# Values and gates of two blocks as 512 wide matmuls over paired weights, and a spread of roots by one product a head

## The chip, the cores and the metric

The kernel runs on one core of a Trainium2 chip. The metric is the device time of one launch in microseconds, lower is better. TensorE multiplies, VectorE and ScalarE empty its PSUM banks and prepare operands, GpSimd takes inverse roots and some sums, and SyncE issues most loads.

## The reference

Two transformer blocks over 512 tokens of width 1024, in float32, one after the other. What the change touches of them:

```python
# first block: gated linear attention (GLA), 4 heads of 256 values, 256 context tokens
q, k, v, r, glr = split(h @ w_in)
o = head_rms_norm(scan forwards + scan backwards)      # per head of 256
y = (o * silu(r)) @ w_out                              # r: the scan gates
# second block: the mixer
u_pool, q, k, v, g = split(rmsnorm(h) @ w_in)
a = pool_mixer(u_pool)
o = retention(rope(q), rope(k), v)                     # 4 heads of 128, chunks of 128
o = o * rsqrt(mean(o * o, axis=-1) + EPS) * gain       # a root per token and head
h = h + concat([a, silu(g) * o]) @ w_out
```

Around these stand the norms, the modulation of the first block and three gated feed-forward layers (width 2816), which take most of the time.

## The kernel before, in words

**Precision by parts.** Each large product is computed from two parts of either operand. ScalarE rounds a raw weight unit w_raw (128 x 8 x 256, slot 0 or 1) to its upper part w_hi (`split_hi`, L1190), VectorE subtracts for the lower part w_lo (`split_lo`, L1606), and activations lie as a_hi and a_lo. `mm3` (L505) issues three matmuls: upper by upper, upper by lower, lower by upper. A matmul here is a weight load of 128 x 128 and the columns that move past it.

**Most units** (`unit`, L526) have the weights stationary and 512 tokens moving, so that the output has features on partitions. **Three kinds have tokens stationary** and 256 features moving, for an output with tokens on partitions: the GLA values (`v_unit`, L696, not changed), the GLA scan gates r (`r_half`, L750) and the mixer's values (L1039 to L1049). A tile is 128 tokens by 256 features: 8 steps k of 3 matmuls of 256 columns, 24 in all. Two tiles share a PSUM bank (512 float32 columns), one in each half.

**Scan gates.** Each of the four heads of GLA is one round of a loop (L806 to L829). TensorE turns the keys, computes tiles 0 and 1 of the gates into bank 2 (`r_half(h, 0)`), the scores, the key products of blocks 0 and 1, tiles 2 and 3 into bank 3 (`r_half(h, 1)`), the key product of block 2, turns the gated output of the head before and computes the output of this one. ScalarE takes the silu of a whole bank into sr (`silu_half`, L1358), both at the end of its round and ahead of `split_hi`; that frees the bank. VectorE multiplies sr into the normed output (`gate_o`, L1900), merges the scores (`merged_scores`, L1878) and carries the states (`states`, L1888), on which TensorE waits ahead of block 2.

**Mixer's values.** TensorE runs ten units of w_in in order: two for the pool input, two for k, two for q, two for v, two for g. After each, VectorE scales or rotates the output in PSUM (`rotate`, L2245: four instructions for each of two banks). VectorE's queue around the values is an order written out by hand (L2270 to L2322): rotate(4), split_lo(1), rotate(5), split_lo(0), the decayed operands of two retention heads (`ret_inputs`, L2281), split_lo(1). rotate(5) belongs to unit 5, the last of q. The values' two units n = 0, 1 fill banks 2n and 2n + 1, two tiles each. Unit 0 waits for rotate(4), unit 1 for rotate(5). ScalarE copies each tile into vr, scaled by the token's root (L1540 to L1547), and splits the next weights behind each unit. TensorE then waits for all eight copies (L1124), computes the scores and turned keys of head 0 and the first of the gate chunks.

**Retention roots.** GpSimd raises the 16 mean squares of a partition (4 heads, 4 token tiles) to the power -1/2 (L482). TensorE spreads them over the partitions by 16 matmuls of 128 columns, with the root as a broadcast stationary operand and the identity moving (L1158 to L1163). They are plain float32, for which the profile shows two passes each. VectorE multiplies them into gr (L2360), ScalarE and VectorE split the result, and TensorE uses it from `mix_part(0, range(4, KD))` on. Elsewhere in the kernel a spread is one matmul of 512 columns: all ones stationary, and moving a row of four diagonals, which VectorE makes (`diagonal`, L1637; `broadcast`, L554).

Of the kernel before, what the change touches and what calls it, by code (L numbers as in the profile page):

```python
# [7 lines left out]
ALU = mybir.AluOpType  # L8
# [113 lines left out]
def build(nc, a):  # L122
    with ExitStack() as ctx:  # L123
# [27 lines left out]
        w_hi = [place(f"w_hi{s}", [P, KD, UC], F32R) for s in range(2)]  # L151
        w_lo = [place(f"w_lo{s}", [P, KD, UC], F32R) for s in range(2)]
# [73 lines left out]
        st = tmp[2]  # L226
        ret_q, ret_k, ret_p = ([tmp[j], dec_k[i]] for i, j in enumerate((0, 1, 3)))
# [31 lines left out]
        masks_set, reset_set = sem("masks_set"), sem("reset_set")  # L259
# [41 lines left out]
        cst_done = sem("context_state_copied")  # L301
        o_hi_done, o_lo_done = sem("o_hi_done"), sem("o_lo_done")
# [189 lines left out]
        def _(pe):  # L492
# [257 lines left out]
            def r_half(h, half):  # L750

                s, b = h % 2, 2 + half
                if half == 0:
                    pe.wait_ge(lo_done[s], cnt.next(lo_done[s]))
                take(b)
                for j in range(2):
                    t = 2 * half + j
                    for k in range(KD):
                        m = mm3(bank[b][:, j * DV:(j + 1) * DV],
                                (a_hi[:, k, t * P:(t + 1) * P], a_lo[:, k, t * P:(t + 1) * P]),  # L760
                                (w_hi[s][:, k], w_lo[s][:, k]), k == 0, k == KD - 1)
                m.then_inc(ready[b], 1)
# [276 lines left out]
            for n in range(2):  # L1039
                pe.wait_ge(lo_done[n], cnt.next(lo_done[n]))  # L1040
                pe.wait_ge(roped, cnt.upto(roped, CPU * (n + 3)))
                for b in (2 * n, 2 * n + 1):
                    for j in range(2):
                        t = 2 * (b % 2) + j
                        for k in range(KD):
                            m = mm3(bank[b][:, j * UC:(j + 1) * UC],
                                    (a_hi[:, k, t * P:(t + 1) * P], a_lo[:, k, t * P:(t + 1) * P]),
                                    (w_hi[n][:, k], w_lo[n][:, k]), k == 0, k == KD - 1)
                    m.then_inc(ready[b], 1)  # L1049
# [108 lines left out]
            pe.wait_ge(root_done, 12)  # L1158
            for h in range(HR):
# [1372 lines left out]
```

## Time and profile before

| | us |
|---|---|
| median of 3 runs | 1614.9 |
| lowest and highest | 1614.07, 1618.32 |
| the profiled execution: its time | 1615.48 |
| its span | 1613.7 |
| TensorE busy in it | 1598.7 (99%) |
| VectorE, ScalarE, GpSimd busy | 843.4, 497.7, 119.8 |
| mean granted clock of TensorE | 0.996 |

The difference between the execution's time and its span lies outside what the engines' records cover. A matmul's row gives a start and a modelled duration, which overlaps the next: the distance of two starts is what one costs. In a timeline a row is start, duration, engine, line, operation, output and inputs, and in brackets the idle time ahead of it with what ended it. A granted clock of 1.00 is 2.4 GHz, 0.50 is 1.2 GHz.

### The profile page before, as it was taken

Reading aid. Unit: us, or ns where it says so; the run is one execution under the profiler, and the core shown is the slowest. Engines: PE = TensorE matmul, PEld = TensorE weight load, DVE = VectorE, ACT = ScalarE, POOL = GpSimd, SP = SyncE. Lnnn points to the kernel's source line nnn. Section 1 sums busy time; section 2 is a strip of 40 time slices with the busy share of each in tenths; the row PEclk is TensorE's granted clock in tenths of the full one; section 3 lists DMA queues with packets and bytes.
Section 4 is the critical chain, followed back from the end, with each engine's and each line's share of the span. In section 5 each row is a group of like instructions: output and inputs, shape, how many; then the busy total and the mean of one; then the engine's idle time right before and its main releaser. Section 6 shows DMA issues by size and latency. Waiting matters only on the chain.

```text
span 1613.7 us, 19892 instructions
## 1 busy us (share of the span) xinstructions
PE 1598.7 (99%) x8095; PEld 1359.1 (84%) x8095; DVE 843.4 (52%) x1032; ACT 497.7 (31%) x571; POOL 119.8 (7%) x106
## 2 busy tenths in 40 slices
PE   8999999999999999999999999999999999999998
PEld 6899999888888888888888888888988888888887
DVE  5897754674334344584544444346457445444444
ACT  4553264532222233441221222321223212222222
POOL 0100000020000000000000003135006000000000
PEclk9999999999999999999999999999999999999999
DMA  9544511212222222322222223332212222222332
GB/s 384 183 167 157 209 53 53 79 61 96 104 104 80 90 88 89 113 85 109 80 102 104 79 84 104 99 144 105 79 53 78 105 104 83 99 104 67 96 98 79
DMA packets 30361, 171.38 MB, mean 106 GB/s; under 512 B 3168, under 2 KB 5472, under 8 KB 16608
## 3 DMA queue, kind: packets, MB, share of 16 engines
q1 hardware_dynamic: 25952, 153.80, 27.3%
q0 software_dynamic: 4352, 16.78, 3.1%
q8 instruction: 41, 0.67, 0.2%
q14 instruction: 16, 0.13, 0.0%
HBM read 168.47 MB, written 2.10 MB: 106 GB/s over the span
## 4 chain that ended last, share of the span: by engine, by line
PE 96%; DMA 2%; DVE 1%; issue 0%; SPq 0%; ACT 0%; POOL 0%; POOLq 0%; DVEq 0%
PE bank L503 95%; DMA mod_w<-in_mod 2%; DVE mod_sum L1629 0%; PE bank L803 0%; SPq L346 0%; PE bank L747 0%; ACT w_hi L1193 0%; PE bank L1072 0%; PE bank L693 0%; SPq L349 0%; DVE y_ffn L2405 0%; ACT tmp L1396 0%; POOL root L408 0%; POOLq L123 0%; DVE qd L1982 0%
## 5 line engine op out<-in xcount | busy, mean ns | idle before, releaser
L1608 DVE TENSOR_TENSOR w_lo<-w_raw,w_hi 128x2048 fp32r<-128x2048 f32 x142 | 327.8, 2308 | 378.1 <-ACT w_hi L1193 378.0
L503 PE MATMUL bank<-a_hi,w_hi 128*128 128x512 f32 x1245 | 486.8, 391 | 0.0
L503 PE MATMUL bank<-a_hi,w_lo 128*128 128x512 f32 x1245 | 484.5, 389 | 0.0
L503 PE MATMUL bank<-a_lo,w_hi 128*128 128x512 f32 x1245 | 484.5, 389 | 0.0
L1193 ACT ACTIVATE w_hi<-w_raw 128x2048 fp32r<-128x2048 f32 x144 | 275.5, 1913 | 556.3 <-PE bank L503 556.1
L503 PEld LDWEIGHTS bank<-a_hi,w_hi 128*128 128x128 f32 x1245 | 233.8, 188 | 49.9 <-issue 1.9
L503 PEld LDWEIGHTS bank<-a_hi,w_lo 128*128 128x128 f32 x1245 | 233.7, 188 | 48.8
L503 PEld LDWEIGHTS bank<-a_lo,w_hi 128*128 128x128 f32 x1245 | 233.8, 188 | 48.1 <-issue 0.5
L503 PE MATMUL bank<-g_hi,w_hi 128*128 128x512 f32 (+1 forms) x544 | 210.4, 387 | 0.0
L503 PE MATMUL bank<-g_lo,w_hi 128*128 128x512 f32 (+1 forms) x544 | 210.0, 386 | 0.0
L503 PE MATMUL bank<-g_hi,w_lo 128*128 128x512 f32 (+1 forms) x544 | 210.0, 386 | 0.0
L503 PEld LDWEIGHTS bank<-g_hi,w_lo 128*128 128x128 f32 x544 | 102.5, 188 | 20.7
L503 PEld LDWEIGHTS bank<-g_lo,w_hi 128*128 128x128 f32 x544 | 102.6, 189 | 20.5
L503 PEld LDWEIGHTS bank<-g_hi,w_hi 128*128 128x128 f32 x544 | 102.6, 189 | 20.4
L503 PE MATMUL bank<-w_hi,a_hi 128*128 128x256 f32 x320 | 91.9, 287 | 0.0
L408 POOL TENSOR_TENSOR root<-col,power 128x4 f32<-128x4 f32 (+2 forms) x15 | 17.3, 1154 | 996.3 <-DVE col L1635 809.7
L503 PE MATMUL bank<-w_hi,a_lo 128*128 128x256 f32 x320 | 90.5, 283 | 0.0
L503 PE MATMUL bank<-w_lo,a_hi 128*128 128x256 f32 x320 | 90.5, 283 | 0.0
L1459 ACT ACTIVATE tmp<-tmp 128x512 f32<-128x512 f32 x44 | 27.7, 632 | 175.9 <-DVE tmp L2137 175.9
L2143 DVE TENSOR_TENSOR tmp<-bank,roots 128x512 f32<-128x512 f32 x44 | 30.4, 692 | 98.4 <-PE bank L503 98.4
L2137 DVE TENSOR_TENSOR tmp<-bank,roots 128x512 f32<-128x512 f32 x43 | 29.5, 688 | 88.1 <-PE bank L503 85.2
L503 PEld LDWEIGHTS bank<-w_hi,a_hi 128*128 128x128 f32 x320 | 61.2, 191 | 0.2
(299 smaller groups left out, 1604.2 us busy)
## 6 DMA issues: line engine op xcount, KB each, us to landing
w_raw<-in_ffn_in SPq DMA_DIRECT2D x66, 1024.0 KB, 4.8
w_raw<-in_ffn_out SPq DMA_DIRECT2D x24, 768.0 KB, 4.2
mod_raw<-in_mod POOLq DMA_DIRECT2D x16, 1024.0 KB, 5.5
w_raw<-in_ffn_out SPq DMA_DIRECT2D x24, 640.0 KB, 3.9
w_raw<-in_gla_in SPq DMA_DIRECT2D x12, 1024.0 KB, 4.8
w_raw<-in_mix_in SPq DMA_DIRECT2D x10, 1024.0 KB, 4.9
mod_w<-in_mod SPq DMA_DIRECT2D x8, 1024.0 KB, 18.8
w_raw<-in_gla_out SPq DMA_DIRECT2D x4, 1024.0 KB, 4.7
```

What stands on the lines that cost most here:

```text
L408: nc.gpsimd.tensor_tensor(root4[:, c0:c0 + n], col4[:, c0:c0 + n], power[:, 0:n], ALU.pow).then_inc(root_done, 1)
L503: return pe.matmul(out, lhs, rhs, start=first, stop=last, skip_group_check=True)
L1193: nc.scalar.activation(flat(w_hi[s]), flat(w_raw[s]), ACT.Copy).then_inc(hi_done[s], 1)
L1459: nc.scalar.activation(tmp[c][:], tmp[c][:], ACT.Silu).then_inc(silu_done, 1)
L1608: V.tensor_tensor(flat(w_lo[s]), flat(w_raw[s]), flat(w_hi[s]).bitcast(F32), ALU.subtract).then_inc(lo_done[s], 1)
L2137: V.tensor_tensor(tmp[c][:], gate, roots[:], ALU.mult).then_inc(gate_scaled, 1)
L2143: V.tensor_tensor(tmp[2 + c][:], bank[2 + c][:], roots[:], ALU.mult).then_inc(up_scaled, 1)
```

## The change

w_hi and w_lo of a slot become the two halves of one tensor, w_two. A new function computes a tile of tokens with two matmuls a step instead of three: the upper activations stationary and 512 columns moving, which are the upper weights' 256 and then the lower weights' 256, and the lower activations stationary with the upper weights' 256 added into the bank's second half. Upper by upper then lies in the first half of a bank and the rest in the second, so that a tile fills a bank. ScalarE copies the first half to SBUF and VectorE adds the second.

The gates use banks 2 and 3 in turn, and tiles wait for VectorE's adds (r_added); the silu runs in SBUF. The values' units use banks 2n and 2n + 1 in turn, and tiles 2 and 3 wait for VectorE's add of tiles 0 and 1 (free). TensorE's wait for the copies of the values goes, and one for the four banks comes behind the first scores. The roots of retention are spread by one product of 512 columns a head, from diagonals that VectorE makes.

```diff
-        w_hi = [place(f"w_hi{s}", [P, KD, UC], F32R) for s in range(2)]
-        w_lo = [place(f"w_lo{s}", [P, KD, UC], F32R) for s in range(2)]
+        w_two = [place(f"w_two{s}", [P, 2, KD, UC], F32R) for s in range(2)]
+        w_hi, w_lo = ([w_two[s][:, j] for s in range(2)] for j in range(2))
...
+            def tile_of_tokens(b, s, t):
+                for k in range(KD):
+                    hi, lo = (x[:, k, t * P:(t + 1) * P] for x in (a_hi, a_lo))
+                    mm(bank[b][:].rearrange("p (w e) -> p w e", w=2), hi, w_two[s][:, :, k], k == 0, False)
+                    m = mm(bank[b][:, UC:2 * UC], lo, w_hi[s][:, k], False, k == KD - 1)
+                return m
...
             def r_half(h, half):
...
-                take(b)
                 for j in range(2):
                     t = 2 * half + j
-                    for k in range(KD):
-                        m = mm3(bank[b][:, j * DV:(j + 1) * DV],
...
-                m.then_inc(ready[b], 1)
+                    if h or t >= 2:
+                        pe.wait_ge(r_added, PAIRS * h + t - 1)
+                    else:
+                        take(2 + j)
+                        filled[2 + j] = False
+                    tile_of_tokens(2 + j, s, t).then_inc(ready[2 + j], 1)
...
             for n in range(4):
...
+                if n == 0:
+                    pe.wait_ge(r_added, PAIRS * HG)
...
-                for b in (2 * n, 2 * n + 1):
-                    for j in range(2):
-                        t = 2 * (b % 2) + j
-                        for k in range(KD):
-                            m = mm3(bank[b][:, j * UC:(j + 1) * UC],
...
-                    m.then_inc(ready[b], 1)
+                for t in range(RCH):
+                    b = 2 * n + t % 2
+                    if t >= 2:
+                        pe.wait_ge(free[b], cnt.next(free[b]))
+                    tile_of_tokens(b, n, t).then_inc(ready[b], 1)
...
-            pe.wait_ge(v_copied, cnt.next(v_copied, 8))
             ret_scores_of(0)
+            for b in range(4):
+                pe.wait_ge(free[b], cnt.next(free[b]))
             gate_chunk(0)
...
             mix_part(1, range(3))
-            pe.wait_ge(root_done, 12)
-            for h in range(HR):
-                for t in range(RCH):
-                    c = RCH * h + t
-                    m = mm(bank[4 + h][:, t * P:(t + 1) * P], root4[:, c:c + 1].to_broadcast([P, P]), ident[:], True, True)
-                m.then_inc(roots_ready, 1)
+            broadcast(4, T, ret_diag[0])
+            broadcast(5, T, ret_diag[1])
             mix_part(1, (3,))
+            broadcast(6, T, ret_diag[2])
+            broadcast(7, T, ret_diag[3])
             mix_part(0, range(4, KD))
...
# ScalarE
+            def upper_half(h, half):
+                for j in range(2):
+                    act.wait_ge(ready[2 + j], cnt.next(ready[2 + j]))
+                    nc.scalar.activation(sr[h % 2][:, 2 * half + j], bank[2 + j][:, 0:DV], ACT.Copy).then_inc(r_left, 1)
...
             def silu_half(h, half):
-                b = 2 + half
-                act.wait_ge(ready[b], cnt.next(ready[b]))
...
+                act.wait_ge(r_added, PAIRS * h + 2 * half + 2)
+                x = sr[h % 2][:, 2 * half:2 * half + 2]
+                nc.scalar.activation(x, x, ACT.Silu)
...
                     middle_decays(h + 1)
+                upper_half(h, 0)
                 block_states(h, 1)
...
                 silu_half(h, 0)
+                upper_half(h, 1)
+                split_hi(h % 2)
                 silu_half(h, 1)
-                split_hi(h % 2)
...
# VectorE
+            def gate_sums(h, half):
+                for j in range(2):
+                    t = 2 * half + j
+                    dve.wait_ge(r_left, PAIRS * h + t + 1)
+                    x = sr[h % 2][:, t]
+                    V.tensor_tensor(x, x, bank[2 + j][:, DV:2 * DV], ALU.add).then_inc(r_added, 1)
...
                     gate_o(h - 1)
+                gate_sums(h, 0)
                 merged_scores(h)
...
                     o_lower(h - 1)
+                gate_sums(h, 1)
                 split_lo(h % 2)
...
             rotate(5)
+            def values_added(n, tiles):
+                for t in tiles:
+                    x = vr[:, t, n * UC:(n + 1) * UC]
+                    b = 2 * n + t % 2
+                    dve.wait_ge(v_copied, cnt.next(v_copied))
+                    V.scalar_tensor_tensor(x, bank[b][:, UC:2 * UC], root4[:, t:t + 1], x, ALU.mult, ALU.add).then_inc(free[b], 1)
+            values_added(0, range(RCH))
             split_lo(0)
...
             ret_inputs(0)
+            values_added(1, (0, 1))
             ret_inputs(1)
+            values_added(1, (2, 3))
             split_lo(1)
...
+            for h in range(HR - 1):
+                diagonal(ret_diag[h], RCH, RCH * h)
             for h in range(HR):
                 dve.wait_ge(roots_ready, cnt.next(roots_ready))
                 V.tensor_tensor(gr[:, h], gr[:, h], bank[4 + h][:], ALU.mult).then_inc(scaled, 1)
-                if h:
+                if h == 0:
+                    diagonal(ret_diag[HR - 1], RCH, RCH * (HR - 1))
+                else:
                     head_lower(h - 1)
```

ScalarE's copies of the values change with the tiles (256 columns from a bank's first half, the same scale). Two semaphores of the mask set-up are replaced by the general step semaphore, with the same waits.

## Rows read from the trace of the kernel before

**Rows 1.** The page: busy time by engine, and the chain's shares by engine

```profile
PE 1598.7 (99%) x8095; PEld 1359.1 (84%) x8095; DVE 843.4 (52%) x1032; ACT 497.7 (31%) x571; POOL 119.8 (7%) x106
...
PE 96%; DMA 2%; DVE 1%; issue 0%; SPq 0%; ACT 0%; POOL 0%; POOLq 0%; DVEq 0%
```

**Rows 2.** The chain in order of time: start, duration, what

```profile
191.98 0.76 DVE mod_sum L1629
...
231.67 15.89 PE bank L503 x124
...
332.73 359.33 PE bank L503 x1584
...
1151.79 1.13 PE bank L503 x8
...
1153.35 7.02 PE bank L503 x38
```

**Rows 3.** TensorE's timeline, the mixer's values: matmuls 1, 2 and 192

```profile
1127.62 0.28 PE L503 MATMUL bank<-w_hi,a_hi 128*128 128x256 f32 x1
1127.73 0.28 PE L503 MATMUL bank<-w_lo,a_hi 128*128 128x256 f32 x1
...
1150.53 0.28 PE L503 MATMUL bank<-w_hi,a_lo 128*128 128x256 f32 x1
```

**Rows 4.** VectorE's timeline beside the mixer's values

```profile
1129.77 2.29 DVE L1608 TENSOR_TENSOR w_lo<-w_raw,w_hi 128x2048 fp32r<-128x2048 f32 x1 [2.81 <-ACT w_hi L1193]
...
1137.15 0.69 DVE L2260 TENSOR_TENSOR qr<-qr,tmp 128x512 f32<-128x512 f32 x1
1142.01 2.29 DVE L1608 TENSOR_TENSOR w_lo<-w_raw,w_hi 128x2048 fp32r<-128x2048 f32 x1 [4.17 <-ACT w_hi L1193]
1144.21 0.69 DVE L2284 TENSOR_TENSOR tmp<-qr,decay 128x512 f32<-128x512 f32 x1
1144.82 0.69 DVE L2284 TENSOR_TENSOR tmp<-kr,decay 128x512 f32<-128x512 f32 x1
```

**Rows 5.** ScalarE's timeline beside the mixer's values

```profile
1127.82 1.92 ACT L1193 ACTIVATE w_hi<-w_raw 128x2048 fp32r<-128x2048 f32 x1 [8.96 <-PE bank L503]
...
1139.33 0.84 ACT L1545 ACTIVATE vr<-bank,root 128x256 f32<-128x256 f32 x2 [4.92 <-PE bank L503]
1140.06 1.91 ACT L1193 ACTIVATE w_hi<-w_raw 128x2048 fp32r<-128x2048 f32 x1
```

**Rows 6.** The tile sr: VectorE's three-operand form (ns: shortest, median, longest)

```profile
L1908 DVE SCALAR_TENSOR_TENSOR sr<-bank,root,sr x16: 472/476/485, 212.8 to 280.1; 128x256 f32<-128x256 f32 x16
```

**Rows 7.** VectorE's timeline, GLA head 1: merged scores, and the last state

```profile
216.43 0.69 DVE L1882 TENSOR_TENSOR tmp<-bank,masks 128x512 f32<-128x512 f32 x1 [1.96 <-PE bank L503]
...
224.35 0.91 DVE L1897 SCALAR_TENSOR_TENSOR u_state<-u_state,small,bank 128x256 f32<-128x256 f32 x2 [2.52 <-PE bank L503]
```

**Rows 8.** ScalarE's timeline, GLA head 1: the gates' silu

```profile
228.27 1.09 ACT L1362 ACTIVATE sr<-bank 128x512 f32<-128x512 f32 x2
```

**Rows 9.** Busy time by stretch: PE, PEld, DVE, ACT, POOL, PEclk, DMA share, GB/s

```profile
697.00:698.00 1.00, 1.00 (x8) 1.00 (x7) 1.00 (x1) 0.00 (x0) 0.00 (x0) 0.66 0.00 0
...
699.00:700.00 1.00, 1.00 (x4) 0.71 (x3) 0.93 (x4) 0.43 (x1) 0.00 (x0) 0.50 0.81 131
700.00:701.00 1.00, 1.00 (x4) 0.80 (x3) 0.84 (x4) 0.29 (x1) 0.72 (x1) 0.64 0.69 279
```

**Rows 10.** TensorE's timeline in the same stretch: 512 wide matmuls

```profile
698.67 0.63 PE L503 MATMUL bank<-g_hi,w_lo 128*128 128x512 f32 x1
699.09 0.63 PE L503 MATMUL bank<-g_hi,w_hi 128*128 128x512 f32 x1
```

**Rows 11.** TensorE's timeline, the spread of the retention roots

```profile
1204.60 3.73 PE L503 MATMUL bank<-ident,root 128*128 128x128 f32 x32
...
1208.40 0.39 PE L503 MATMUL bank<-m_lo,w_hi 128*128 128x512 f32 x1
```

**Rows 12.** GpSimd's timeline, the retention roots

```profile
1200.92 2.91 POOL L408 TENSOR_TENSOR root<-col,power 128x16 f32<-128x16 f32 x1 [89.43 <-DVE col L2350]
```

More of the change, by code:

```diff
@@ L226, in build @@
         st = tmp[2]
+        ret_diag = tmp
         ret_q, ret_k, ret_p = ([tmp[j], dec_k[i]] for i, j in enumerate((0, 1, 3)))
@@ L750, in r_half @@
             def r_half(h, half):
-                s, b = h % 2, 2 + half
+                s = h % 2
                 if half == 0:
                     pe.wait_ge(lo_done[s], cnt.next(lo_done[s]))
-                take(b)
                 for j in range(2):
                     t = 2 * half + j
-                    for k in range(KD):
-                        m = mm3(bank[b][:, j * DV:(j + 1) * DV],
-                                (a_hi[:, k, t * P:(t + 1) * P], a_lo[:, k, t * P:(t + 1) * P]),
-                                (w_hi[s][:, k], w_lo[s][:, k]), k == 0, k == KD - 1)
-                m.then_inc(ready[b], 1)
+                    if h or t >= 2:
[4 more added lines that the diff above has]
+                    tile_of_tokens(2 + j, s, t).then_inc(ready[2 + j], 1)
             def scores(h):
@@ L1356, in o_upper @@
                     nc.scalar.activation(o_hi[2 * h + e][:], bank[4 + e][:], ACT.Copy, scale=col("gla_g", e)).then_inc(o_hi_done, 1)
+            def upper_half(h, half):
+                for j in range(2):
+                    act.wait_ge(ready[2 + j], cnt.next(ready[2 + j]))
+                    nc.scalar.activation(sr[h % 2][:, 2 * half + j], bank[2 + j][:, 0:DV], ACT.Copy).then_inc(r_left, 1)
             def silu_half(h, half):
-                b = 2 + half
-                act.wait_ge(ready[b], cnt.next(ready[b]))
-                nc.scalar.activation(sr[h % 2][:, 2 * half:2 * half + 2], bank[b][:].rearrange("p (t e) -> p t e", t=2),
-                                     ACT.Silu).then_inc(free[b], 1)
+                act.wait_ge(r_added, PAIRS * h + 2 * half + 2)
+                x = sr[h % 2][:, 2 * half:2 * half + 2]
+                nc.scalar.activation(x, x, ACT.Silu)
             act.wait_ge(small_exp, 1)
@@ L1540, in _ @@
             for n in range(2):
-                for b in (2 * n, 2 * n + 1):
+                for t in range(RCH):
+                    b = 2 * n + t % 2
                     act.wait_ge(ready[b], cnt.next(ready[b]))
-                    for j in range(2):
-                        t = 2 * (b % 2) + j
-                        nc.scalar.activation(vr[:, t, n * UC:(n + 1) * UC], bank[b][:, j * UC:(j + 1) * UC], ACT.Copy,
-                                             scale=root4[:, t:t + 1]).then_inc(v_copied, 1)
+                    nc.scalar.activation(vr[:, t, n * UC:(n + 1) * UC], bank[b][:, 0:UC], ACT.Copy,
+                                         scale=root4[:, t:t + 1]).then_inc(v_copied, 1)
                 split_hi(n)
@@ L1764, in _ @@
             split_lo(1)
-            V.tensor_tensor_scan(masks[:, 0], one[:, 0:1].to_broadcast([P, P]), ident[:], 0.0, ALU.mult, ALU.add).then_inc(masks_set, 1)
-            V.tensor_tensor(masks[:, 1], ones[:], ident[:], ALU.add).then_inc(masks_set, 1)
-            dve.wait_ge(masks_set, 1)
-            V.tensor_tensor(masks[:, 0], masks[:, 0], ident[:], ALU.subtract).then_inc(masks_set, 1)
-            V.memset(reset[:], 1.0).then_inc(reset_set, 1)
-            dve.wait_ge(reset_set, 1)
-            V.memset(reset[:].rearrange("p (t q) -> p t q", q=BLK)[:, :, 0:1], 0.0).then_inc(reset_set, 1)
-            dve.wait_ge(reset_set, 2)
+            V.tensor_tensor_scan(masks[:, 0], one[:, 0:1].to_broadcast([P, P]), ident[:], 0.0, ALU.mult, ALU.add).then_inc(dve_step, 1)
+            V.tensor_tensor(masks[:, 1], ones[:], ident[:], ALU.add)
+            dve.wait_ge(dve_step, cnt.next(dve_step))
+            V.tensor_tensor(masks[:, 0], masks[:, 0], ident[:], ALU.subtract)
+            V.memset(reset[:], 1.0).then_inc(dve_step, 1)
+            dve.wait_ge(dve_step, cnt.next(dve_step))
+            V.memset(reset[:].rearrange("p (t q) -> p t q", q=BLK)[:, :, 0:1], 0.0).then_inc(dve_step, 1)
+            dve.wait_ge(dve_step, cnt.next(dve_step))
             def log_gates(i):
```

5 lines of the change are left out of this document (2 added, 3 removed).

## The prediction

> **What bounds the kernel now.** I read the page first: TensorE is busy 99% of the span and holds 96% of the chain that ended last [rows 1]. A cheaper TensorE instruction therefore shortens the run one for one, except where TensorE waits, and every new wait of TensorE lengthens it unless other work covers it. Next the chain in order of time, for the rate of a long undisturbed stretch and for the places where the chain leaves TensorE [rows 2]: in GLA head 0 it runs over VectorE's modulation sums (mod_sum), and behind the mixer's values TensorE waits before its next matmul. Last the timelines of TensorE, VectorE and ScalarE around the mixer's values [rows 3 to 5]: what decides there is the order of VectorE's queue.
>
> All sums are against the profiled execution's own 1615.48 us (span 1613.7). The median of the runs shown is 1614.9, 0.6 lower; I quote medians by adding to 1614.9. The runs shown spread over 4 us, so about 0.3%, 4.8 us, is what a measurement can tell from no change.
>
> **Step 1, what one tile of tokens costs.** Before, a tile takes 24 matmuls of 256 columns. In the values they start every 0.120 us: from the second at 1127.73 to the 192nd at 1150.53 are 190 steps in 22.80 us [rows 3]. A 512 wide one costs 359.33/1584 = 0.2268 us [rows 2]. After, a tile is 8 x (0.2268 + 0.120) = 2.77 us instead of 2.88: 0.104 saved. No columns go away (768 per k either way); what goes is one fixed cost per k, 2 x 0.120 - 0.2268 = 0.013 us. Bounds for the form that no row shows, 512 columns read as two blocks of 256: 0.2268, or 0.240 if it pays the fixed cost twice (saving nothing). I take the first, since one instruction and one weight load are issued.
>
> The Trainium skill, "TensorE: Matmul & The Clock Gate", section "Wait — 56ns, not 53.3ns?", puts the fixed cost of a warm matmul at about 2.5 ns beyond its columns. By that rule a tile saves 8 x 2.5 = 20 ns instead of 104, and the 22 tiles that count 0.4 us instead of 2.3, which would put the median at 1620.9. The rows here speak against it: 0.120 and 0.2268 us are both 13 ns over their columns at 2.4 GHz.
>
> **Step 2, the scan gates (16 tiles).** Two tiles, head 0's first half, save nothing: behind them TensorE waits for the modulation sums anyway [rows 2]. 14 x 0.104 = 1.46 us saved. What is added per head: four ScalarE copies of 256 columns out of PSUM, four VectorE adds of 256 columns, and the silu now reads SBUF in two pieces as before. Copies cost 0.37 each behind one another (two vr copies start at 1139.33, the next instruction at 1140.06) [rows 5]; adds at most the 0.476 of the three-operand form [rows 6]. Are they covered? First half: TensorE fills banks 2 and 3, then does scores and key products (some 3.5 us) before tile 2 wants bank 2 back, and the adds need under 1.5. VectorE's adds stand ahead of the merged scores, where it idles 1.96 us in head 1 [rows 7], so the scores come perhaps 0.7 us later (ScalarE itself is some 1.5 late by then: two copies of the previous head and two of this one). The states then end 0.7 late; VectorE stands idle 2.52 us between them and the next key product [rows 7], so TensorE, 0.4 sooner by its own saving, still finds them ready. Second half: the silu piece starts at 228.27 [rows 8], copies last till about 229.5, adds till 230.0, and the next head's tiles begin at 231.67, or 0.4 sooner [rows 2]. Covered: cost 0. If the cover were gone it would cost what the slack lacks, under 1 us a head.
>
> **Step 3, the mixer's values (8 tiles).** 8 x 0.104 = 0.83 us saved. TensorE's wait for all eight copies goes: from 1150.65 (the last values matmul's turn ends) to 1151.79 is 1.14 us [rows 2, 3]. The next wait, for the four banks, comes after the first head's scores and turned keys, 1.56 us of TensorE work; the last copy and add need 0.20 + 0.46 + 0.48 = 1.14, so it is covered.
>
> But each tile now fills a bank, and **tile 2 may start only when VectorE has added tile 0**. Where do these adds stand in VectorE's queue? Behind the rotation of the last q unit. ScalarE's upper part of the next weights starts when unit 5 is out (1127.82) and ends at 1129.7 [rows 5], VectorE then splits it (1129.77, 2.29 us), then rotates, and the last rotation instruction starts at 1137.15; VectorE is free at 1137.8 [rows 4]. All of this hangs on the end of unit 5, as does TensorE's start on the values at 1127.62, so the distance is rigid. TensorE is through tiles 0 and 1 at 1127.62 + 5.55 = 1133.17. The first add runs 1137.77 to 1138.25, and TensorE goes on at 1138.3. **Stall: 5.1 us**, uncovered, because the only TensorE work left is in the queue behind it. Tile 3's bank comes 0.4 later and is covered by tile 2.
>
> For the second unit there are fresh banks for two tiles. Let E be the end of the first unit's tile 3. Its copy starts at E + 0.20 (1139.33, where by the pitch the 96th matmul's turn ends at 1139.13), ScalarE's split follows at E + 0.57, VectorE's starts 1.95 later (1140.06 to 1142.01) and holds it 2.20, then come two decayed operands at 0.61 each (1144.21 to 1144.82): VectorE reaches the second unit's first add at E + 5.94 and ends it at E + 6.42 [rows 4, 5]. TensorE wants bank 2 at E + 5.55. **Second stall 0.9 us.** The last two adds stand behind two more operands and are in time.
>
> Sum of step 3 at full clock: -0.83 - 1.14 + 5.1 + 0.9 = +4.0, and 0.1 for starting again after the long gap: **+4.1**.
>
> **Step 4, the clock.** Full clock is granted throughout the values now. Where TensorE does little, it is not: behind the sums of a norm the granted share falls to 0.50 (1.2 of 2.4 GHz); by the shares of the microseconds at its ends, 0.66 and 0.64, it is low from 697.3 to 700.7 [rows 9], and 512 wide matmuls start every 0.43 us instead of 0.2268 [rows 10]. That stretch cost 3.4 x (1 - 0.2268/0.43) = 1.6 us. The 5.1 us stall is barer than that, so I expect a fall. Bounds: 0 (the stall itself eats the low stretch, or no fall), and 3.2 (two such stretches). Part of the low time may lie in the stall, so I take 1.5.
>
> **Step 5, the retention roots.** 16 plain matmuls of 128 columns (32 passes, from 1204.60 to 1208.17, that is 1208.40 less one turn: 3.57 us) [rows 11] become 4 of 512: the same columns in 8 passes. A pass of 128 takes 0.1116, two cycles of 2.4 GHz a column (0.1067) and a rest of 0.005 us; with the rest paid 8 times instead of 32 it is 3.45. Gain at most 0.16, with no rest at all. VectorE has the first diagonal 0.7 us after the roots (one 512 wide product, 0.69 as L2284's) [rows 4], and the roots end at 1200.92 + 2.91 = 1203.83 [rows 12], so it comes at about 1204.6, when TensorE does. The diagonals 1 and 2 follow at 0.6 each, under the products; the fourth stands behind the first scaling and has tile products of 1.4 us as cover. The head scalings come some 1 us later for heads 2 and 3, needed only 2.7 and 4.1 us after the last spread. I take 0, bounds -0.2 and +0.5. The semaphores renamed in the masks cost nothing: the same waits at the same places.
>
> **Sum.** -1.46 (gates) + 4.1 (values) + 1.5 (clock) + 0 (roots) = +4.1 us: 1619.6 in a profile, **1619.0 as a median**, +0.26%. That is just inside what can be told from no change.
>
> **Rivals.**
> - **The stall at full clock**: no fall, or a fall wholly inside the gap. +2.6: 1617.5. For it: full clock was kept over the 1.14 us gap. Against it: the low share came without such a gap [rows 9]. 0.12.
> - **The low clock lasts** (the slower side): TensorE returns in pieces, two tiles and another gap of 0.9, and the granted share stays at 0.50 for two such stretches [rows 9], so 3.2 instead of 1.5 us: +5.8, 1620.7. It decides the verdict from 2.2 us of clock cost on. 0.13.
> - **Paid twice**: the 512 wide form over two blocks takes 0.240, so 22 tiles on the path save nothing (2.29 us back): 1621.3. 0.05.
> - **No stall**: the change does not hold TensorE as I read it, or VectorE is earlier. Then -1.46 - 0.83 - 1.14 + 0.9 = -2.5: 1612.4. Against it: the wait on the bank is a wait on VectorE's add, and its place behind the rotation is in the code. 0.06.
> - **A gate wait**: ScalarE's extra copies make merged scores and states late enough in heads 1 and 2 that TensorE waits, 0.7 us each past the slack: +5.5, 1620.4. 0.04.
>
> **How the numbers follow.** My forecast has 0.60; its own spread (clock 0.6 to 2.6, restart and gaps 0.3) is 1618 to 1620.5, and a quarter of it (0.15) lies above 1619.7, where slower by over 0.3% begins. Slower: 0.15 + 0.13 + 0.05 + 0.03 = 0.36. Faster by over 0.3% needs under 1610.1, which no case reaches: 0.02. The rest, 0.62, is within 0.3%. The range leaves out the no-stall case and the far end of the slower ones: 1615.0 to 1621.7.
>
> **What would show it.** In the changed profile: a TensorE gap of 5 us in the values, ended by VectorE's add of the values, and one of 0.9 in the second unit; a granted share of 0.5 in the microseconds behind the first; no gap before the first head's scores; values and gate tiles with 16 instead of 24 matmuls, 2.77 us apart; TensorE's chain whole through heads 1 to 3. A first gap under 3 us, or gate tiles that wait for VectorE, would make the prediction wrong.

## The result, and the profile after

| | before | after |
|---|---|---|
| median of 7 runs each, us | 1616.26 | 1621.45 |
| lowest and highest | 1614.07, 1618.91 | 1620.52, 1624.77 |
| ratio, with its 95% interval | 1 | 1.0042 (1.0033 to 1.0052) |
| the profiled execution: its time | 1615.48 | 1621.36 |
| its span | 1613.7 | 1618.6 |

The change makes the kernel slower by 0.42% by the ratio, 6.8 us of 1616 with 5.3 to 8.4 as its interval; the medians of seven alone are 5.2 us apart, and launches of one kernel spread over 4 to 5 us. The forecast of 1619.0, reckoned from a median of 1614.9 before, had it at +0.26%, within 0.3%. The median lies in the range (1615.0 to 1621.7), near its upper end.

The page after, busy time by engine and the chain's shares, to be held against [rows 1]:

```profile
PE 1598.9 (99%) x7879; PEld 1347.5 (83%) x7879; DVE 855.3 (53%) x1060; ACT 502.8 (31%) x587; POOL 119.8 (7%) x106
...
PE 95%; DMA 2%; DVE 1%; ACT 1%; issue 1%; SPq 0%; POOL 0%; POOLq 0%; DVEq 0%
```

TensorE issues 216 matmuls fewer (8 in each of 24 tiles, and 24 passes of the roots) and is busy as long as before: what the wide form saves, something gives back. Its share of the chain is a point lower. The chain in order of time shows where (start, duration, what), to be held against [rows 2]:

```profile
194.29 13.59 PE bank L504 x68
...
208.75 15.57 PE bank L504 x92
...
231.26 15.48 PE bank L504 x92
...
270.12 12.02 PE bank L504 x54
...
1125.57 1.93 ACT w_two L1200
...
1135.59 0.41 DVE vr L2308
...
1136.04 8.56 PE bank L504 x32
...
1150.87 6.81 PE bank L504 x40
...
1158.12 7.20 PE bank L504 x38
```

In GLA the chain stays on TensorE and its pieces are shorter: 15.57 and 15.48 for 15.89. In the mixer's values it leaves TensorE at the end of unit 5, runs over ScalarE's and VectorE's parts of the next weights and the rotations to VectorE's sum of the values, and comes back at 1136.04. TensorE's timeline there (start, duration, engine, line, operation, output and inputs, idle before and its releaser):

```profile
1125.37 0.39 PE L504 MATMUL bank<-w_two,a_hi 128*128 128x512 f32 x1
...
1130.89 0.28 PE L504 MATMUL bank<-w_two,a_lo 128*128 128x256 f32 x1
1136.04 0.80 PE L504 MATMUL bank<-w_two,a_hi 128*128 128x512 f32 x1 [4.87 <-DVE vr L2308]
1136.63 0.41 PE L504 MATMUL bank<-w_two,a_lo 128*128 128x256 f32 x1
...
1137.27 0.41 PE L504 MATMUL bank<-w_two,a_lo 128*128 128x256 f32 x1
...
1149.85 0.27 PE L504 MATMUL bank<-w_two,a_lo 128*128 128x256 f32 x1
1150.87 0.50 PE L504 MATMUL bank<-w_two,a_hi 128*128 128x512 f32 x1 [0.75 <-DVE vr L2308]
```

and VectorE's, with the split, the last rotation, and the sums behind them:

```profile
1127.52 2.29 DVE L1621 TENSOR_TENSOR w_two<-w_raw,w_two 128x2048 fp32r<-128x2048 f32 x1 [2.81 <-ACT w_two L1200]
...
1134.89 0.69 DVE L2283 TENSOR_TENSOR qr<-qr,tmp 128x512 f32<-128x512 f32 x1
1135.50 0.87 DVE L2308 SCALAR_TENSOR_TENSOR vr<-bank,root,vr 128x256 f32<-128x256 f32 x2
...
1150.34 0.87 DVE L2308 SCALAR_TENSOR_TENSOR vr<-bank,root,vr 128x256 f32<-128x256 f32 x2
```

Both gaps end where VectorE has its sum. TensorE started the values at 1125.37 and tile 2 at 1136.04, 10.67 us later; the prediction had 1138.3 less 1127.62, which is 10.68. The idle times in brackets (4.87 and 0.75) count from a matmul's modelled end. Counted from the end of its turn, 0.12 us behind its start, as the prediction counts, the stalls are 1136.04 - 1131.01 = 5.0 and 1150.87 - 1149.97 = 0.9 us.

Behind the first gap a step k, one wide and one narrow matmul, takes 0.64 us (1136.63 to 1137.27) where it took 0.35. The busy time by stretch says why (columns as in [rows 9]):

```profile
1135.00:1136.00 1.00, 0.00 (x0) 0.00 (x0) 1.00 (x3) 0.00 (x0) 0.00 (x0) 0.60 0.00 0
...
1141.00:1142.00 1.00, 1.00 (x5) 0.81 (x5) 0.00 (x0) 0.44 (x1) 0.00 (x0) 0.50 0.00 0
1142.00:1143.00 1.00, 1.00 (x7) 0.87 (x7) 0.48 (x1) 0.04 (x1) 0.00 (x0) 0.99 0.00 0
```

The granted share falls to 0.50, 1.2 of 2.4 GHz, at about 1135.2 (0.60 in that microsecond), and is back at 1142.0: 6.8 us, of which only the first 0.8 lie in the gap.

Two stretches of the chain hold the account. **GLA**, from the piece at 194.29 to the one at 270.12, takes 75.83 us. Before, it took 77.06, from 194.19 to 271.25; its first piece there and the one that follows the stretch were

```profile
194.19 13.79 PE bank L503 x84
...
271.25 12.01 PE bank L503 x54
```

so GLA is 1.23 shorter. **The values**, from their first matmul to the end of the piece of 38 matmuls: before, 1127.62 [rows 3] to 1153.35 + 7.02 = 1160.37 [rows 2], 32.75 us; after, 1125.37 to 1158.12 + 7.20 = 1165.32, 39.95 us. That is 7.20 longer. The retention roots: the two pieces of the chain behind the values, ahead of the roots, last 17.33 and 8.84 in both kernels, and the roots themselves take what they took (below). -1.23 + 7.20 = +6.0 us, inside the interval of the ratio (5.3 to 8.4 us). The two spans differ by 4.9 us only: between the two stretches the kernel before took 856.4 us and the changed one 855.3, and before had a granted clock of 0.66 from 324 to 328 where the changed one had 1.00. Behind the values both take 453.3 us to the end of the span. I use these two stretches for all kernels below, since they don't depend on what the clock did elsewhere in an execution.

### The profile page after: what moved, and what is told of

It reads as the page before. It is cut to its first block, busy times and chain, and to the rows that moved or that the text cites. A ratio compares the mean times of both kernels' runs of the same rounds, so it can differ in the third digit from the quotient of the medians.

```text
span 1618.6 us, 19505 instructions
## 1 busy us (share of the span) xinstructions
PE 1598.9 (99%) x7879; PEld 1347.5 (83%) x7879; DVE 855.3 (53%) x1060; ACT 502.8 (31%) x587; POOL 119.8 (7%) x106
## 4 chain that ended last, share of the span: by engine, by line
PE 95%; DMA 2%; DVE 1%; ACT 1%; issue 1%; SPq 0%; POOL 0%; POOLq 0%; DVEq 0%
PE bank L504 94%; DMA mod_w<-in_mod 2%; ACT w_two L1200 0%; DVE mod_sum L1642 0%; SPq L347 0%; PE bank L812 0%; PE bank L756 0%; DVE w_two L1621 0%; POOL root L409 0%; PE bank L1080 0%; PE bank L702 0%; SPq L350 0%; DVE qr L2281 0%; DVE qr L2283 0%; DVE tmp L2279 0%
## 5 line engine op out<-in xcount | busy, mean ns | idle before, releaser
L504 PE MATMUL bank<-a_hi,w_two 128*128 128x512 f32 x2490 | 772.7, 390 | 0.0
L504 PEld LDWEIGHTS bank<-a_hi,w_two 128*128 128x128 f32 x2490 | 467.4, 188 | 98.5 <-issue 1.5
L1621 DVE TENSOR_TENSOR w_two<-w_raw,w_two 128x2048 fp32r<-128x2048 f32 x142 | 327.7, 2308 | 361.1 <-ACT w_two L1200 361.0
L504 PE MATMUL bank<-a_lo,w_two 128*128 128x512 f32 x1245 | 484.4, 389 | 0.0
L1200 ACT ACTIVATE w_two<-w_raw 128x2048 fp32r<-128x2048 f32 x144 | 275.5, 1913 | 555.3 <-PE bank L504 555.1
L504 PE MATMUL bank<-g_hi,w_two 128*128 128x512 f32 (+1 forms) x1088 | 331.9, 386 | 0.0
L504 PEld LDWEIGHTS bank<-a_lo,w_two 128*128 128x128 f32 x1245 | 233.8, 188 | 48.3 <-issue 0.5
L504 PEld LDWEIGHTS bank<-g_hi,w_two 128*128 128x128 f32 x1088 | 203.8, 189 | 41.4
L504 PE MATMUL bank<-g_lo,w_two 128*128 128x512 f32 (+1 forms) x544 | 210.0, 386 | 0.0
L504 PE MATMUL bank<-w_two,a_hi 128*128 128x256 f32 (+1 forms) x448 | 118.1, 340 | 5.6 <-DVE vr L2308 5.6
```

Source lines behind the costliest of these rows:

```text
L504: return pe.matmul(out, lhs, rhs, start=first, stop=last, skip_group_check=True)
L1200: nc.scalar.activation(flat(w_hi[s]), flat(w_raw[s]), ACT.Copy).then_inc(hi_done[s], 1)
L1621: V.tensor_tensor(flat(w_lo[s]), flat(w_raw[s]), flat(w_hi[s]).bitcast(F32), ALU.subtract).then_inc(lo_done[s], 1)
```

## The experiments

Time is judged by the ratio to the kernel before, measured beside it. In the diffs "-" is the changed kernel, and for e2, e6, e7 and e10 the kernel that the text names.

| kernel | ratio (95%) | GLA stretch | values stretch |
|---|---|---|---|
| changed, as given | 1.0042 (1.0033 to 1.0052) | 75.83 | 39.95 |
| e8, changed, again | 1.0042 (1.0029 to 1.0055) | 77.51 * | 39.81 |
| e1, first order | 1.0000 (0.9990 to 1.0010) | 77.55 * | 32.09 |
| e2, both orders | 0.9990 (0.9981 to 0.9999) | 77.60 * | 31.04 |
| e11, both orders, again | 0.9985 (0.9976 to 0.9994) | 75.83 | 31.03 |
| e3, gap filled | 1.0032 (1.0020 to 1.0044) | 75.93 | 37.24 |
| e9, gap half filled | 1.0027 (1.0018 to 1.0036) | 77.60 * | 37.23 |
| e5, a bank for each tile | 0.9993 (0.9984 to 1.0003) | 77.78 * | 31.14 |
| e4, values as before | 1.0000 (0.9989 to 1.0010) | 75.92 | 32.75 |
| e6, e2 with roots as before | 0.9991 (0.9982 to 1.0000) | 77.46 * | 31.34 |
| e7, e2 with gates as before | 0.9994 (0.9985 to 1.0003) | 78.67 * | 31.01 |
| e10, e2 with two narrow matmuls | 0.9994 (0.9985 to 1.0003) | 77.06 | 31.73 |

\* the clock was low for a while in head 0 in this execution (0.79 granted from 192 to 200, against 1.00): 1.6 to 1.8 us by the first piece of the chain (15.21 to 15.36 against 13.59).

### The changed kernel again (e8)

> The changed kernel itself, once more and beside the others. By its earlier measurement a ratio to before of 1.0033 to 1.0052; a profile with a gap of 4.9 us ahead of the values' tile 2 ended by VectorE's sum and a granted clock near 0.50 for the 6 us behind it. If the low clock behind the gap is chance, it may be absent or of half the length here; if the gap makes it, it is there again for 6 to 7 us.

TensorE's timeline at tile 2 of the first unit:

```profile
1137.65 0.79 PE L504 MATMUL bank<-w_two,a_hi 128*128 128x512 f32 x1 [4.86 <-DVE vr L2308]
```

and the busy time by stretch at both ends of the low clock:

```profile
1136.00:1137.00 1.00, 0.00 (x0) 0.00 (x0) 0.97 (x2) 0.00 (x0) 0.00 (x0) 0.70 0.00 0
...
1143.00:1144.00 1.00, 1.00 (x6) 0.88 (x6) 0.31 (x1) 0.47 (x1) 0.00 (x0) 0.88 0.00 0
```

Gap, ratio and low clock are there again. In between every microsecond has 0.50; by the shares at the ends it is low from 1136.4 to 1143.2, 6.8 us as before. So it is no accident of one execution, and e3 and e9 below show that it belongs to the gap.

### The first order in VectorE's queue (e1)

```diff
             rotate(4)
-            split_lo(1)
             rotate(5)
...
-            values_added(0, range(RCH))
+            values_added(0, (0, 1))
+            split_lo(1)
+            values_added(0, (2, 3))
             split_lo(0)
```

> The lower part of the weights for unit 5's slot partner (2.2 us of VectorE) is moved from before the last q rotation to behind the first two sums of the values; nothing else. My theory: the loss of the changed kernel is the stall of 4.87 us that VectorE's queue makes ahead of tile 2, plus the low clock behind it (0.50 granted from 1135.2 to 1142.0, some 2.7 us lost). So the gap shrinks to under 3 us or goes, the granted clock stays at 1.00 through the values, and the time falls by 5 to 7.6 us against the changed kernel: about 1614, ratio to before 0.9985 to 1.000. The second gap (0.75) stays or shrinks. Rival 'the form': the wide tiles, gates or roots hold the loss, and the order gives back 2.2 us at most (what was moved). Rival 'clock alone is chance': the gap goes and 5 us come back, but a low stretch stays somewhere in the values.

The weights whose lower part is moved are those of the second values unit, which TensorE wants only four tiles later.

VectorE's timeline of e1 behind the last rotation:

```profile
1133.94 0.48 DVE L2307 SCALAR_TENSOR_TENSOR vr<-bank,root,vr 128x256 f32<-128x256 f32 x1
1135.25 0.48 DVE L2307 SCALAR_TENSOR_TENSOR vr<-bank,root,vr 128x256 f32<-128x256 f32 x1 [0.83 <-ACT vr L1558]
1135.65 2.28 DVE L1621 TENSOR_TENSOR w_two<-w_raw,w_two 128x2048 fp32r<-128x2048 f32 x1
```

and TensorE's at the second gap:

```profile
1146.59 0.50 PE L504 MATMUL bank<-w_two,a_hi 128*128 128x512 f32 x1 [0.75 <-DVE vr L2307]
```

The values start at 1128.90 in this execution, so the first sum ends at 1134.4, 5.5 us later, where it was 10.6 in the changed kernel. More than the 2.2 us of the split is gained because in the changed kernel the split itself waited for ScalarE (2.81 idle in the row at 1127.52), and the rotation of both banks behind it. TensorE is through its two tiles after 5.65 and does not wait; the granted clock is 1.00 in the whole stretch; only the second gap is left. The values stretch is 39.95 - 32.09 = 7.9 us shorter and the ratio goes from 1.0042 to 1.0000. One split in the wrong place is the whole loss. The rival "the form", which gave the order 2.2 us at most, falls.

### Both orders (e2, e11)

On top of e1:

```diff
+            values_added(1, (0,))
             ret_inputs(0)
-            values_added(1, (0, 1))
+            values_added(1, (1,))
```

> The first experiment's order, and the first sum of the second unit ahead of the first head's decayed operands instead of behind them. My theory: the second gap (0.75 us at 1150.87 in the changed kernel) goes too and nothing else changes, so 0.7 to 0.8 less than the first experiment: about 1613.2, ratio to before 0.997 to 0.999. Rival: the decayed operands are now late and TensorE waits ahead of the first scores of the retention, so the 0.75 only moves; then it equals the first experiment.

VectorE's timeline of e2, the second unit's first sums around two decayed operands:

```profile
1142.75 0.48 DVE L2307 SCALAR_TENSOR_TENSOR vr<-bank,root,vr 128x256 f32<-128x256 f32 x1
1143.14 0.68 DVE L2318 TENSOR_TENSOR tmp<-qr,decay 128x512 f32<-128x512 f32 x1
1143.74 0.69 DVE L2318 TENSOR_TENSOR tmp<-kr,decay 128x512 f32<-128x512 f32 x1
1144.34 0.48 DVE L2307 SCALAR_TENSOR_TENSOR vr<-bank,root,vr 128x256 f32<-128x256 f32 x1
```

No gap is left in the values, and none appears ahead of the scores. The stretch is 1.05 shorter than e1's, 1.7 shorter than the kernel before's. That is more than the 0.75 expected: counted from the end of a turn the gap was 0.9, and the first matmul behind it took 0.34 us where others take 0.23.

> The kernel of the second experiment once more, beside the one with narrow matmuls, and to settle whether it beats the kernel before. By the trace it saves 1.2 us in the gates and 1.9 in the values: 3.1 us, ratio 0.998. By its first measurement, 0.9981 to 0.9999. If the low clock behind other gaps (it fell in some launches and not in others) moves with the change, the gain may be smaller than the trace's; expected 0.9980 to 0.9992.

Twice the interval lies below 1 (0.9981 to 0.9999, 0.9976 to 0.9994): this version beats the kernel before, by 1.6 and 2.4 us, and the changed one by more. The two stretches give 1.2 + 1.7 = 2.9 us, which lies in both intervals.

### The gap filled, and half filled (e3, e9)

```diff
+                    if n == 0 and t == 2:
+                        keep_busy(7, 22)
                     if t >= 2:
                         pe.wait_ge(free[b], cnt.next(free[b]))
```

> 22 plain matmuls of 128 columns (some 4.8 us, their output in a bank that is not in use) are put into TensorE's queue ahead of tile 2's wait, so the gap is filled and TensorE waits as long as before for VectorE's sum. My theory: the gap alone lowers the clock, so the granted clock stays at 1.00 from 1135 to 1142 and tile 2 and 3 run at 0.35 us a step k instead of 0.64: 2.7 us less than the changed kernel, if tile 2 starts at 1136.0 as in it: about 1618.8. This measures the clock term of the sum by itself (I had taken 1.5). Rival: the low clock there comes from what happened earlier (phase of the throttle) and not from the gap; then it is low all the same and the time does not change.

TensorE's timeline of e3, the filler (44 passes) and tile 2, and then the busy time of the microsecond in which tile 2 starts:

```profile
1131.14 5.08 PE L504 MATMUL bank<-ident,ones 128*128 128x128 f32 x44
1136.16 0.50 PE L504 MATMUL bank<-w_two,a_hi 128*128 128x512 f32 x1
1136.50 0.28 PE L504 MATMUL bank<-w_two,a_lo 128*128 128x256 f32 x1
...
1136.85 0.28 PE L504 MATMUL bank<-w_two,a_lo 128*128 128x256 f32 x1
```

```profile
1136.00:1137.00 1.00, 1.00 (x7) 0.78 (x7) 0.50 (x2) 0.00 (x0) 0.00 (x0) 1.00 0.00 0
```

Tile 2 starts as late as before, but a step k takes 0.35 us. The stretch is 39.95 - 37.24 = 2.71 us shorter. That is the clock term by itself, but for 0.1 us of slightly faster tiles at the end. The ratio fell by 0.0010, 1.6 us; the intervals take in 2.7, and overlap, so that the ratio alone would not tell it from nothing.

For e9, the same with `keep_busy(7, 10)`:

> As the experiment that fills the gap ahead of tile 2, but with 10 plain matmuls (some 2.2 us) instead of 22, so that TensorE idles for the last 2.6 us or so before tile 2. The whole gap of 4.9 us gave a low clock for 6 to 7 us (cost 2.7), the filled one none. Theory A: what counts is how long TensorE idles at a stretch, and 2.6 us gives half of it, one stretch of 3.4 us: cost about 1.4 us, ratio to before 1.0035 to 1.004. Theory B: any such gap gives the full 6.8 us: ratio as the changed kernel's, 1.0042. Theory C: 2.6 us is too short and the clock stays at 1.00, as over the 1.14 us gap of the kernel before: ratio as with the filled gap, 1.0032.

The same two views of e9 (20 passes):

```profile
1132.59 2.40 PE L504 MATMUL bank<-ident,ones 128*128 128x128 f32 x20
1137.61 0.50 PE L504 MATMUL bank<-w_two,a_hi 128*128 128x512 f32 x1 [2.63 <-DVE vr L2310]
```

```profile
1138.00:1139.00 1.00, 1.00 (x7) 0.87 (x6) 0.00 (x0) 0.00 (x0) 0.00 (x0) 1.00 0.00 0
```

and its chain for tiles 2 and 3, which was 8.56 in the changed kernel:

```profile
1137.61 5.93 PE bank L504 x32
```

2.63 us of idleness leave the clock at 1.00, and the stretch equals e3's (37.23). So theory C holds for a gap of this length, here; gaps between 2.6 and 4.9 us were not tried. A trace shows each filled gap in one execution only. The mean granted clock over whole launches agrees: it is at most 0.996 in all 12 launches of the changed kernel (with e8), and 0.997 or more in 14 of the 17 of e3 and e9.

### A bank for each tile (e5)

```diff
-                    b = 2 * n + t % 2
-                    if t >= 2:
-                        pe.wait_ge(free[b], cnt.next(free[b]))
+                    b = VAL_BANKS[n][t]      # ((0, 1, 4, 5), (2, 3, 6, 7))
                     tile_of_tokens(b, n, t).then_inc(ready[b], 1)
...
+            for b in (0, 1, 4, 5):
+                pe.wait_ge(free[b], cnt.next(free[b]))
             ret_scores_of(0)
-            for b in range(4):
+            for b in (2, 3):
                 pe.wait_ge(free[b], cnt.next(free[b]))
             gate_chunk(0)
+            for b in (6, 7):
+                pe.wait_ge(free[b], cnt.next(free[b]))
```

> VectorE's queue as in the changed kernel, but each of the eight tiles of the values has a bank of its own, so no tile waits for a sum; the waits for the banks stand ahead of the first scores and around the first gate chunk. My theory: what held TensorE was the late sum in VectorE's queue, by way of the bank; without that tie the order of the queue costs nothing, no gap and no low clock: as the experiment with both orders changed, 7.5 to 8.4 us below the changed kernel, ratio to before 0.998 to 0.9995. Rival: the sums' lateness turns up ahead of the first scores, a gap of 1 to 5 us there; then it lies between the two.

VectorE's queue is the changed kernel's, sums behind the split and the rotations, and no matmul of the stretch waits: 31.14 us, against 31.04 with both orders changed. So a late sum cost nothing here once no tile needed its bank.

### One part undone at a time (e4, e6, e7)

The values' code of the kernel before, in the changed kernel (e4), on TensorE, and with it ScalarE's copies; VectorE's sums go:

```diff
-                for t in range(RCH):
-                    b = 2 * n + t % 2
-                    if t >= 2:
-                        pe.wait_ge(free[b], cnt.next(free[b]))
-                    tile_of_tokens(b, n, t).then_inc(ready[b], 1)
+                for b in (2 * n, 2 * n + 1):
+                    for j in range(2):
+                        t = 2 * (b % 2) + j
+                        for k in range(KD):
+                            m = mm3(bank[b][:, j * UC:(j + 1) * UC],
...
+            pe.wait_ge(v_copied, cnt.next(v_copied, 8))
             ret_scores_of(0)
-            for b in range(4):
-                pe.wait_ge(free[b], cnt.next(free[b]))
```

> The mixer's values are computed, copied and waited for as in the kernel before; the gates and the roots stay changed. My theory: the whole loss is in the values (7.0 us in the chain between 1125.4 and 1158.1), so the time is 7.0 below the changed kernel and 1.2 below the kernel before, which is the gates' gain: ratio to before 0.9992. Rival 'gates hurt too' or 'roots hurt': it stays above the kernel before. Rival of my first sum: gates gain 1.46 or more.

The values stretch is the old one, 32.75, and GLA's keeps its gain. The ratio 1.0000 is above the 0.9992 expected, which lies in its interval, and the whole loss is gone.

The spread of the roots as before, in e2 (e6); VectorE's diagonals go:

```diff
-            broadcast(4, T, ret_diag[0])
-            broadcast(5, T, ret_diag[1])
+            pe.wait_ge(root_done, 12)
+            for h in range(HR):
+                for t in range(RCH):
+                    c = RCH * h + t
+                    m = mm(bank[4 + h][:, t * P:(t + 1) * P], root4[:, c:c + 1].to_broadcast([P, P]), ident[:], True, True)
+                m.then_inc(roots_ready, 1)
             mix_part(1, (3,))
-            broadcast(6, T, ret_diag[2])
-            broadcast(7, T, ret_diag[3])
```

> Both orders changed as in the second experiment, and the retention roots spread as in the kernel before (16 products of 128 columns in place of 4 of 512). My theory: roots are worth 0 (the stretches of the chain on both sides of them were equal to 0.01 us in both kernels), so the time is the second experiment's within 0.3 us. Rival: the new spread gained 0.16 us or lost up to 0.5; the first can't be told from nothing.

0.9991 against 0.9990 and 0.9985: no difference that the measurement tells. (Its values stretch is 0.3 longer than e2's, although the roots lie behind it: all its eight tiles there have the slower of the two paces told below, in e2 only the first two.) In the changed kernel the four spreads lie in two pairs, and what each takes is read from the next product:

```profile
1209.57 1.98 PE L504 MATMUL bank<-tmp,ones 128*128 128x512 f32 x4
...
1211.63 0.40 PE L504 MATMUL bank<-m_lo,w_two 128*128 128x512 f32 x1
...
1212.79 1.88 PE L504 MATMUL bank<-tmp,ones 128*128 128x512 f32 x4
...
1214.73 0.39 PE L504 MATMUL bank<-m_lo,w_two 128*128 128x512 f32 x1
```

1211.63 less one turn (0.23) less 1209.57 is 1.83, and 1214.73 - 0.23 - 1212.79 is 1.71: 3.54 us, where the 16 narrow ones took 3.57.

The gates as before, in e2 (e7): `r_half` and `silu_half` of the kernel before, without `upper_half`, `gate_sums` and the wait for the last sums behind the loop over heads:

```diff
-                    tile_of_tokens(2 + j, s, t).then_inc(ready[2 + j], 1)
+                    for k in range(KD):
+                        m = mm3(bank[b][:, j * DV:(j + 1) * DV],
...
-                gate_sums(h, 0)
...
-                gate_sums(h, 1)
...
-                upper_half(h, 0)
...
-                upper_half(h, 1)
```

> Both orders changed as in the second experiment, and the scan gates computed, copied and silu'd as in the kernel before. My theory: the gates give 1.2 us (my sum had 1.46, the chain through GLA is shorter by 1.2), so this is 1.2 above the second experiment: about 1614.3, ratio to before 0.999 to 1.000. Rival: the gates give nothing or cost, and the second experiment's gain is all from the values; then it is the same or below.

The chain of e7 in GLA, one of the three pairs of halves:

```profile
234.75 15.89 PE bank L504 x124
```

It is back at 15.89 with 124 matmuls. The GLA stretch is 78.67 against 77.60 in e2's execution (both with the low clock in head 0): 1.1. By the ratio it is 0.0004 to 0.0009 above the two runs of the same kernel with the new gates, 0.6 to 1.5 us. The gates' gain is real in the trace; the ratios alone would not tell it from nothing.

### The form by itself (e10)

```diff
-                    mm(bank[b][:].rearrange("p (w e) -> p w e", w=2), hi, w_two[s][:, :, k], k == 0, False)
+                    mm(bank[b][:, 0:UC], hi, w_hi[s][:, k], k == 0, k == KD - 1)
+                    mm(bank[b][:, UC:2 * UC], hi, w_lo[s][:, k], k == 0, False)
```

Here two sums are open in one bank at once. The engines' work is the same. The start of the second sum clears what marks the first as begun (the Trainium skill, "PSUM — Partial Sum Buffer", section "The four PSUM rules": a group's first matmul clears these marks for the whole bank). By that rule, which no trace here can show, this kernel leaves the upper products of the first step k out of its output.

> Both orders changed as in the second experiment, and in every tile of gates and values the 512 wide matmul over both halves is issued as two of 256 columns: same columns, same banks, same waits, 24 matmuls instead of 16. It prices the form by itself. My sum had 0.104 us a tile, 22 tiles on the path: 2.3 us more than the second experiment. The paces in the profiles since (0.347 to 0.354 us a step k in the new form against 0.360) give 0.05 to 0.10 a tile: 1.1 to 2.3 more, about 1614.9. Rival: the form gives nothing, and what the gates and values gained came from waits alone: then it equals the second experiment.

The chain of e10, the same pair:

```profile
231.55 15.89 PE bank L504 x124
```

A tile takes 2.88 us again. Against e11, measured beside it and with the clock alike in GLA, the GLA stretch is 77.06 - 75.83 = 1.23 longer and the values' 31.73 - 31.03 = 0.70: 1.9 us for the form, and 1.5 us by the medians (1613.57, 1612.03), though the intervals of the two ratios overlap. The rival "the form gives nothing" falls. With narrow matmuls GLA takes exactly the kernel before's 77.06 and the pieces the same 15.89: the new banks, copies and sums of the gates cost nothing.

## Why the prediction was right or wrong

The forecast failed in its verdict, within 0.3% where +0.42% came, and by a size, not a mechanism. Its sum was +4.1 us; the trace gives +6.0. Of the 1.9 between them about 1.2 are the clock, 0.4 the values at full clock and 0.2 the gates.

**Step 4, the clock, is the term that was mis-sized.** It took 1.5 us; by e3 it is 2.7. I had priced one low stretch of 3.4 us as in [rows 9], part of it inside the stall. It lasted twice that, 6.8 us in two executions, and all but 0.8 and 1.2 us of it lay behind the stall, at 0.64 instead of 0.35 us a step. The nearest row for its price was a place where TensorE did products of one column (128x1) and waited 0.3 us at most; in the trace of before its longest wait was 3.3 us, so nothing showed how long the clock stays down after one of 5. The bound of 3.2 held it. The rival "the low clock lasts" had the size, two such stretches, and the right verdict, but a wrong reason: TensorE did not return in pieces. It ran tiles 2 and 3 back to back, and the second gap came at 1150, nearly nine microseconds after the clock was back.

**Step 3, the values at full clock**, was +4.1; with the gap filled (e3) it is 37.24 - 32.75 = +4.5. The order of VectorE's queue, the place of the sum in it and the end of the stall, 10.67 us behind the start, came out as worked, and e1 and e5 show from two sides that the queue and the shared bank made the stall. The two stalls, counted alike, were 5.0 and 0.9 us for 5.1 and 0.9 (5.0 and 0.8 in e3). What made up the 0.4: the tiles saved 0.6 in e3 instead of 0.83 (below), TensorE lost 0.1 in starting again behind each gap and not only behind the first, and the piece behind the first scores grew from 7.02 to 7.20. That growth I had not counted; its cause was not looked for, and it was 7.05 in e5, where other banks are waited for there.

**Steps 1 and 2, the form.** I had 0.104 us a tile. What the new form saves comes in two sizes. The narrow matmuls of one tile of GLA head 3, the first and the eighth, in e2:

```profile
255.15 0.28 PE L504 MATMUL bank<-w_two,a_lo 128*128 128x256 f32 x1
...
257.62 0.28 PE L504 MATMUL bank<-w_two,a_lo 128*128 128x256 f32 x1
```

and those of the same head's last tile:

```profile
267.09 0.27 PE L504 MATMUL bank<-w_two,a_lo 128*128 128x256 f32 x1
...
269.51 0.28 PE L504 MATMUL bank<-w_two,a_lo 128*128 128x256 f32 x1
```

Seven steps take 2.47 us in one and 2.42 in the other, 0.353 and 0.346 each, against 2.52 in every tile of e10. So 8 x 0.013 or 8 x 0.007: 0.10 or 0.05 a tile. The gates gave 1.23 for the 1.46 forecast. "Paid twice" (no saving at all) is out. e10 measured 1.9 us over 22 tiles, 0.088 a tile. The 2.5 ns a matmul of the Trainium skill ("TensorE: Matmul & The Clock Gate", section "Wait — 56ns, not 53.3ns?") would leave 0.02 a tile; the measurement does not bear it out for these matmuls. The cover of the gates held: the merged scores of head 1 start at 216.26, no later than in [rows 7], and VectorE still idles 2.28 us ahead of the last state. "A gate wait" didn't come.

**Step 5, the roots**, 0, was right (3.54 against 3.57 us, and e6).

**"No stall" and "the stall at full clock"** are out by the rows of the gap and of the clock.

**The chances.** The forecast put 0.60 on its own case and three quarters of that within 0.3%. The error was to take a middle value for the clock between bounds of 0 and 3.2 although the sum stood 0.7 us from where slower begins: with +4.1 before any clock cost and -1.46 for the gates, 2.2 us of clock was all that separated the two verdicts, and nothing in the rows spoke for the middle more than for the upper bound. That the median fell into the range all the same owes something to the range's width, not to the clock term.

## What to carry to other kernels

When a change makes tiles share a bank by way of an engine's copy or sum, look up where that sum stands in the engine's queue, before counting what the matmuls save: here 1.9 us of savings hung on one 2.2 us instruction that wasn't urgent and stood ahead of one that was. Here a gap of TensorE of 5 us cost its length and 2.7 us more for the low clock behind it, one of 2.6 us its length alone, and the order of VectorE's queue alone turned the loss into a small gain.

## What was not expected of the hardware

- After 4.9 us without a matmul the granted share was 0.50 for 6.8 us, in both executions in which it was seen, although TensorE was busy without a break for the last 5.6 to 6 of them; after 2.63 us (e9) it was 1.00 throughout.
- One form of matmul has two paces, 0.353 and 0.346 us a step, from tile to tile in one execution. It stays so for whole tiles, and the narrow form shows only 0.360. What chooses between them was not found: in e3 the values' first six tiles had the slower pace, in e6 all eight (and in e5, in other banks), in e1 and e2 only the first two, with the same instructions. In GLA it was the first two tiles of heads 1 and 3 in the changed kernel, in e2 and in e11 alike.
- Launches of one kernel differ by where the clock is low, and no two kernels' profiles need agree in it. In head 0 of GLA it was low in seven of thirteen profiled executions and not in the other six:

```profile
192.00:196.00 4.00, 3.18 (x15) 2.66 (x15) 2.68 (x9) 0.00 (x0) 0.00 (x0) 0.79 0.67 209
```

in e2, and 1.00 in the same stretch of the changed kernel, for the same busy time of TensorE. It costs 1.8 us there (pieces of 15.36 and 13.59). The same holds behind the sums of the two norms, near 326 and 697. Among the executions of the kernel before, those with a mean granted clock of 0.994 took 1618.3 and those with 0.998 1614.5. That is most of a launch's spread, and why a difference of 1 us is read from stretches of the chain rather than from medians.
